# A decoder step with a mixture of experts on one core: bias sums and resident biases, samples and router in four column parts

## The reference, cut to what matters

```
proj = x @ w_in                              # queries, keys, values of two groups of 8 heads
o    = attention of both groups, each head RMS-normed and scaled
hx   = LayerNorm(alpha * x + o @ w_out) * ln1_g + ln1_b
logits = hx @ w_router + b_router            # 32 experts, the 4 best, softmax over their logits: comb
for each expert e:
    gu   = hx @ w_gate_up[e] + b_gate_up[e]          # 1024 x 2048
    act  = clamp(gate) * sigmoid(1.702 * gate) * (clamp(up) + 1)
    acc += comb[:, e] * (act @ w_down[e] + b_down[e]) # 1024 x 1024
y = LayerNorm(alpha * hx + acc) * ln2_g + ln2_b
```

## Time and profile before

| | |
|---|---|
| median of three executions | 1180.72 us |
| the profiled execution | 1180.89 us, of which the span is 1178.8 us |
| TensorE busy | 1121.9 us, 95% of the span |
| VectorE, ScalarE, GpSimd busy | 289.7, 203.8, 30.1 us |
| bytes moved | 454.21 MB, 385 GB/s over the span |
| mean granted TensorE clock | 0.99 of 2.4 GHz |

### The profile page before, as it was taken

One profiled execution on the slowest core, in us unless ns is written; L12 is line 12 of the kernel. 1 busy time (PEld: TensorE's weight loads), 2 busy tenths in 40 slices (PEclk: granted clock), 3 DMA queues, 4 the chain that ended last, 5 costly groups with the idle time before them and its releaser, 6 DMA issues.

```text
span 1178.8 us, 14219 instructions
## 1 busy us (share of the span) xinstructions
PE 1121.9 (95%) x5374; PEld 457.7 (39%) x5375; DVE 289.7 (25%) x707; ACT 203.8 (17%) x479; POOL 30.1 (3%) x65
## 2 busy tenths in 40 slices
PE   7999999899999999999999999999999999999986
PEld 6876764533333333333332323233333333333322
DVE  1543747602121211303030303030303030303113
ACT  1322412402020202021111111111111111111111
POOL 0110111000000000000000000000000000000001
PEclk9999999899999999999999999999999999999998
DMA  9857779668999999999999999999999999999992
GB/s 361 324 197 254 269 270 384 257 263 341 423 428 427 427 428 428 429 428 428 428 428 428 428 428 428 428 427 428 429 428 428 428 428 428 428 428 428 413 424 108
DMA packets 83399, 454.21 MB, mean 385 GB/s; under 512 B 7147, under 2 KB 20099, under 8 KB 36132
## 3 DMA queue, kind: packets, MB, share of 16 engines
q1 hardware_dynamic: 80866, 440.97, 90.5%
q0 software_dynamic: 1728, 10.75, 2.5%
q10 hardware_dynamic: 770, 2.03, 0.4%
HBM read 450.19 MB, written 11.93 MB: 392 GB/s over the span
## 4 chain that ended last, share of the span: by engine, by line
PE 65%; DMA 26%; SPq 5%; ACT 2%; DVE 1%; issue 1%
DMA ring<-in_w_gate_up 23%; PE bank L1083 19%; PE bank L1125 15%; PE bank L968 5%; PE bank L664 5%; PE bank L687 5%; SPq L445 3%; PE bank L851 3%; PE bank L690 2%; DMA ring<-in_w_down 2%; PE bank L1150 2%; PE bank L964 1%; SPq L455 1%; PE bank L804 1%; ACT xtok L1313 1%; ACT actT L1313 1%
## 5 line engine op out<-in xcount | busy, mean ns | idle before, releaser
L1083 PE MATMUL bank<-ring,xg 128*64 128x512 f32 x1904 | 422.8, 597 | 23.8 <-DMA ring<-in_w_gate_up 23.8
L1083 PEld LDWEIGHTS bank<-ring,xg 128*64 128x64 f32 x1904 | 132.0, 137 | 304.8 <-issue 252.3
L1125 PE MATMUL bank<-ring,actT 128*64 128x512 f32 x960 | 215.9, 597 | 3.8 <-ACT actT L1313 3.8
L1930 DVE TENSOR_TENSOR acc<-acc,bank 128x512 f32<-128x512 f32 x60 | 41.2, 687 | 509.3 <-PE bank L1150 509.3
L1458 ACT ACTIVATE sig<-gate 128x256 f32<-128x256 f32 x64 | 26.7, 416 | 545.6 <-DVE gate L1912 545.6
L1125 PEld LDWEIGHTS bank<-ring,actT 128*64 128x64 f32 x960 | 66.6, 137 | 121.5 <-issue 118.7
L1912 DVE TENSOR_SCALAR gate<-bank 128x256 f32<-128x256 f32 x64 | 26.8, 419 | 179.0 <-PE bank L1083 157.3
L687 PE MATMUL bank<-xT,wblk 128*128 128x288 f32 x256 | 67.1, 417 | 1.4 <-DMA wblk<-in_w_in 1.4
L1450 ACT ACTIVATE xg<-bank,small 128x128 f32<-128x128 f32 x128 | 48.1, 458 | 99.1 <-PE bank L664 99.1
L968 PE MATMUL bank<-hx,pick 128*128 128x512 f32 x128 | 61.6, 626 | 0.0
L1150 PE MATMUL bank<-ybuf,spread 128*128 128x512 f32 x120 | 58.3, 618 | 0.0
(11 more groups left out here) (245 smaller groups left out, 716.8 us busy)
## 6 DMA issues: line engine op xcount, KB each, us to landing
ring<-in_w_gate_up SPq DMA_DIRECT2D x119, 2048.0 KB, 29.2
ring<-in_w_down SPq DMA_DIRECT2D x63, 2048.0 KB, 31.5
ring<-in_w_gate_up SPq DMA_DIRECT2D x16, 1024.0 KB, 18.3
wblk<-in_w_in SPq DMA_DIRECT2D x12, 1024.0 KB, 7.4
kring<-in_cache_k_moba SPq DMA_DIRECT2D x16, 256.0 KB, 5.2
vring<-in_cache_v_moba SPq DMA_DIRECT2D x16, 256.0 KB, 5.0
out<-in_state_k_win POOLq DMA_DIRECT2D x8, 512.0 KB, 4.3
out<-in_state_v_win POOLq DMA_DIRECT2D x8, 512.0 KB, 4.9
```

The lines of the kernel that those rows point to most:

```text
L1083: ins = nc.tensor.matmul(bank[n][64 * e:64 * e + 64, :], xg[:, k, 64 * e:64 * e + 64], w[:, 2048 * e + 512 * n:2048 * e + 512 * n + 512], ...
L1125: ins = nc.tensor.matmul(bank[4 + half][64 * e:64 * e + 64, :], actT[:, j, 64 * e:64 * e + 64], w[:, at:at + 512], start=(j == 0), stop=(j ...
L1930: V.tensor_tensor(o, o, new, ALU.add).then_inc(S.added, 1)
```

## The change

The samples' value and out products go in four column parts. In `project` and as `out_samples`, which takes the place of `out_product` for the samples:

```
+                    for q in range(4):
+                        w = wblk[:, (b - 1 + q // 2) % 3, k, 128 * (q % 2):128 * (q % 2) + 128]
+                        ins = nc.tensor.matmul(out[NS * q:NS * q + NS, 256:384], xT[:, k, SEQ:T], w, start=(k == 0),
+                                               stop=(k == KC - 1), tile_position=(0, NS * q))
...
+        def out_samples(k):
+            for q in range(4):
+                ins = nc.tensor.matmul(bank[5][NS * q:NS * q + NS, 0:256], outT[:, k, SEQ:T],
+                                       wout[:, k, 256 * q:256 * q + 256], start=(k == 0), stop=(k == KC - 1),
+                                       tile_position=(0, NS * q))
+            return ins
```

ScalarE copies three of the four parts (`upper`), and VectorE's `v_rows` and `raw_sum` take four pieces instead of two. The router multiplies with its own columns as the stationary operand, in four column strips whose sum a second product with a stacked identity makes (`E` is 32):

```
+        def logits_parts(nth):
...
             for k in range(KC):
                 if k % 4 == 0:
                     pe.wait_ge(S.hxT_ready, 2 * nth + k // 4 + 1)
...
+                r = slice(E * (k % 4), E * (k % 4) + E)
+                ins = nc.tensor.matmul(bank[5][r, 128:128 + rows], wrt[:, k, :], outT[:, k, t0:t0 + rows], start=(k < 4),
+                                       stop=(k >= 4), tile_position=(0, E * (k % 4)))
+            ins.then_inc(S.parted, 1)
...
+        def logits_product(nth):
+            rows = TILES[ORDER[nth]][1]
+            pe.wait_ge(S.parts_ready, nth + 1)
+            nc.tensor.matmul(bank[5][0:rows, E * nth:E * nth + E], parts[:, 0:rows], keep[:, C_EYE:C_EYE + E], start=True,
+                             stop=True).then_inc(S.routed, 1)
...
+        def take_parts(nth):
+            rows = TILES[ORDER[nth]][1]
+            dve.wait_ge(S.parted, nth + 1)
+            V.tensor_copy(parts[:, 0:rows], bank[5][:, 128:128 + rows]).then_inc(S.parts_ready, 1)
```

The first pair's turned rows are awaited block by block, in the banks 6 and 7 in this order:

```
         def turn_slots(i, a):
-            pe.wait_ge(S.xtok_ready, i * 2 + 2)
+            early = isinstance(i, int) and i == 0
+            pe.wait_ge(S.xtok_ready, 1 + a if early else i * 2 + 2)
...
-                if isinstance(i, int) and i == 0 and k == 0:
+                if early:
+                    pe.wait_ge(*((S.xg_ready, k // 4 + 1) if k % 4 == 3 else (S.first_slots, 3 * (k // 4) + k % 4 + 1)))
+                if early and k == 0:
```

All biases of gate/up are loaded once, 32 rows for each of four column blocks, ahead of `load_v(3)`; `load_bias` and `next_bias` are gone. A pair's two rows are picked by the stationary operand, which VectorE writes for each pair, behind `pick_slots`:

```
+        for n in range(4):
+            sp.dma_start(bias_rows[E * n:E * n + E, :], b_gate_up[0, :, 512 * n:512 * n + 512]).then_inc(S.bias_in, 16)
...
+            pe.wait_ge(S.selected, i + 1)
             for n in range(4):
...
+                r = slice(E * n, E * n + E)
+                ins = nc.tensor.matmul(bank[n][:, :], sel[r, :], bias_rows[r, :], start=True, stop=False,
+                                       tile_position=(E * n, 0))
...
+        def select(i, p):
+
+            if not isinstance(i, int) or i > 0:
+                dve.wait_ge(S.bias_used, i)
+            V.tensor_copy(sel[:, :].rearrange("p (e s) -> p e s", e=2),
+                          eye[:, pair_of(p)].unsqueeze(2).broadcast_to([128, 2, SLOTS])).then_inc(S.selected, 1)
```

`select(0, 0)` stands ahead of `router_consts`. The second load of `ln_g` moves ahead of unit 9:

```
+        sp.wait_ge(S.added, 5)
+        sp.dma_start(ln_g[:, :], ln2_g[0:1, :].broadcast_to([128, D])).then_inc(S.ln2_in, 16)
         load_units(0, 0, range(9, UNITS))
-        sp.wait_ge(S.sums_scaled, 6)
-        sp.dma_start(ln_g[:, :], ln2_g[0:1, :].broadcast_to([128, D])).then_inc(S.ln2_in, 16)
-        next_bias(0)
```

```
-        gate_up(0, 0, 0, {1: turn_comb, 4: lambda: add_biases(0), 5: lambda: add_biases(1), 6: add_sample_biases})
+        gate_up(0, 0, 0)
...
+        def finish_with_biases(i, m, odd):
+
+            def first_slots():
+                turn_slots(i + 1, 0)
+                turn_comb()
+
+            def other_slots():
+                pe.wait_ge(S.actT_ready, i * 2 + 2)
+                turn_slots(i + 1, 1)
+                for j in range(2):
+                    add_biases(j)
+
+            def other_biases():
+                for j in range(2, 4):
+                    add_biases(j)
+                add_sample_biases()
+
+            gather(i + 1, i * 2)
+            turn_weights(i, i * 2 + 3)
+            turn_act(i, i * 2 + 4)
+            down(i, m, odd, {0: first_slots, 1: other_slots, 2: other_biases})
```

`add_biases(j)` is now one product of 33 rows and 512 columns into bank j; `add_sample_biases` waits for VectorE's first two sums and issues its eight products in two runs of four column strips. On ScalarE `take_comb` stands behind `take_turned(14)`. On VectorE, ahead of `add_mixed(14)`:

```
+        dve.wait_ge(S.added, 5 * PAIRS - 5)
+        add_biases()
+        dve.wait_ge(S.bias_added, 5)
```

More of the change, by code:

```diff
@@ L69, in constant_tables @@
     keep[:, C_ONE:C_ONE + 128] = 1
[L70 to L73, removed]
+    keep[:, C_IOTA:C_EYE] = np.arange(CHUNKS * SLOTS)
+    keep[p, C_EYE + p % E] = 1
     keep[p, C_HEAD + p // DS % H] = 1
@@ L167, in build_layer @@
     ln_gs, ln_bs = place("ln_gs", [128, 256]), place("ln_bs", [128, 256])
+    late_at = cursor[0]
+    parts = spread[:, 0:128]
     samp_x = place("samp_x", [NS, D])
+    bdn = hx[64:64 + E + 1, 2, :]
+    combT = place("combT", [128, T], at=late_at)[64:64 + E + 1, :]
     wrt = place("wrt", [128, KC, E], at=share_at)
@@ L294, in v_at @@
     def v_at(slot):
-        return sum((3 if n // 2 % 6 == 5 and n % 2 else 1) for n in range(slot + 1) if is_v(n))
+        return sum((5 if n // 2 % 6 == 5 and n % 2 else 1) for n in range(slot + 1) if is_v(n))
     def slot_of_tile(g, kind, j):
@@ L880, in out_part @@
                 pe.wait_ge(S.kstage_ready, 6)
-                out_first(2, range(4))
+                for k in range(4):
+                    out_samples(k)
         for slot in range(STEPS):
@@ L992, in _ @@
         for k in range(4, KC):
-            for half in range(2):
-                ins = out_product(2, half, k)
+            ins = out_samples(k)
         ins.then_inc(S.attended, 1)
@@ L1014, in _ @@
         ins.then_inc(S.attended, 1)
+        logits_parts(1)
+        out_product(1, 1, 4)
         logits_product(1)
-        for k in range(4, KC):
+        for k in range(5, KC):
             ins = out_product(1, 1, k)
@@ L1053, in add_sample_biases @@
-            ins.then_inc(S.spread_down, 1)
+            for q in range(4):
+                r, c = slice(NS * q, NS * q + NS), slice(256 * q, 256 * q + 256)
+                ins = nc.tensor.matmul(bank[1][r, 0:256], combT[:, SEQ:T], bdn[:, c], start=True, stop=True,
+                                       tile_position=(64, NS * q))
+            ins.then_inc(S.bias_sums, 1)
         def gather(i, turned_before):
@@ L1429, in _ @@
         act.wait_ge(S.attended, 1)
-        copy(upper[:, :], bank[5][NS:2 * NS, :]).then_inc(S.upper_ready, 1)
+        for q in range(1, 4):
+            copy(upper[:, q - 1, :], bank[5][NS * q:NS * q + NS, 0:256]).then_inc(S.upper_ready, 1)
         for nth in range(2):
@@ L1746, in raw_sum @@
             dve.wait_ge(S.attended, (2 + half, 4 + half, 1)[t])
[L1747 to L1748 removed]
+            if t == 2:
+                for q in (2 * half, 2 * half + 1):
+                    if q:
+                        dve.wait_ge(S.upper_ready, q)
+                    c = slice(256 * q, 256 * q + 256)
+                    o = upper[:, q - 1, :] if q else bank[5][0:NS, 0:256]
+                    ins = V.scalar_tensor_tensor(hx[0:n, t, c], hx[0:n, t, c], ALPHA, o, ALU.mult, ALU.add)
+                ins.then_inc(S.hx_raw, 1)
+                return
             c = slice(512 * half, 512 * half + 512)
[L1750 to L1751 removed]
+            V.scalar_tensor_tensor(hx[0:n, t, c], hx[0:n, t, c], ALPHA, bank[2 * t + half][:, :], ALU.mult,
+                                   ALU.add).then_inc(S.hx_raw, 1)
         def moments(nth, half):
```

184 lines of the change are left out of this document (79 added, 105 removed).

## The result

| | before | after |
|---|---|---|
| median, us | 1180.72 (1180.22 to 1181.76) | 1173.88 (1171.90 to 1174.39, 4 runs) |
| ratio to before | | 0.9938, 95% interval 0.9922 to 0.9953 |
| profiled execution, us | 1180.89 | 1174.04 |
| span, us | 1178.8 | 1172.1 |

The change brings 6.8 us, where 20.0 were forecast: 1173.9 against 1160.9, and outside the range of 1157 to 1167.

The account below looks back on a forecast made before the run. The weight stream was taken as the bound, with TensorE critical up to 244.4 us and through freed buffers to about 290; -9.2 - 6.0 - 1.2 - 5.2 + 1.6 = -20.0 us from 1180.9 gave 1160.9 us, range 1157 to 1167.

Parts of the forecast that it names:

- (a) to (f): Rivals: VectorE front 0.15, loop's turn 0.08, late work uncaught 0.07, full-clock gather 0.08, lower clock 0.02, stream gap stays 0.03.
- no stretch under 420 GB/s: Sign for the weight stream: from the issue of unit 9 to the last pair it never runs below 420 GB/s.
- part 3: Front: router product in column parts, counts placed later; the first full gather comes 2.0 us earlier.
- part 5: Pair 0: bias sums taken out, buffers free earlier, the stream's gap at 275 to 295 us closes: -6.0 us.
- Part 1: Front: samples' value product in four column parts, done twice, -3.4 us; a skill-based estimate gave 2.8 us.
- Part 2: Front: samples' out product in four parts, worth 0 since TensorE then waits for VectorE; two new holes.
- Part 4: Pair 0: first gate/up block needs one activation instead of all eight, starting about 1.1 us behind the gather: -3.2 us.
- The clock: TensorE's front: shorter hole gives the first block -1.1, new holes slow a full product +0.5: sum -0.6 us.
- rival (d): Front: TensorE's clock stays at 2.4 GHz through the gather, 6.12 becomes 3.7 us, total 1158.5 us; chance 0.08.
- Part 6: Stream: ln_g's load moved ahead of unit 9, -1.2 us; small bias loads gone, 15 x 0.35 = -5.2 us.
- Part 7: Pair 14 and tail: 5.2 us of moved TensorE work, 3.6 caught up in its waits: +1.6 us.
- The two tests named at the end of the prediction: The forecast is wrong if unit 9 is issued after 240 us, or the block 7 to 2 pitch stays at 34.65.

Follow-up runs that it names:

- a1: The changed kernel with 128 unused bytes ahead of the ring, so that its buffers start on multiples of 256 bytes: 1158.95 us.
- b3: a1 with ten products of 512 columns that nobody reads put behind blocks 4, 5 and 6 of pair 0: 1166.72 us.
- a4: a1 with the four two-row loads of a pair put back, into rows that nobody reads: 1163.61 us.
- c1: a1 with the samples' value product in two column parts, as before the change: 1162.82 us.
- b1: a1 with the samples' out product in two column halves, as before the change: 1158.92 us.
- c3: a1 with the router's product whole again and the counts of the known tiles ahead of the gather: 1160.25 us.
- b2: a1 with the first gate/up product of pair 0 waiting for all eight activations again: 1163.64 us.
- b4: a1 with the turned weights and bias sums moved from pair 14 to pair 7: 1157.87 us.
- c2: a1 with ring buffers 0 to 3 on multiples of 256 bytes and 4 to 7 put 128 bytes past one: 1163.02 us.
- c4: a1 with one unread product of 512 columns in each of TensorE's two holes behind the samples' out product: 1158.88 us.

## Why the prediction was wrong

The step that failed is a sentence in the first part that was carried through all others: "19.60 / 4 = 4.90 us for 2 MB", used again as "seven units before it, 34.3 us at 4.90" for the kernel after. The pitch was taken to be a property of the chip and of the load's shape. It also depends on where the buffers start, and the change moved them. Nothing in the trace of before could show that price, but its cause stood in the diff, in declarations that were passed over and so costed at zero without a word. None of the rivals (a) to (f) had it. Nor could the sign named for the stream catch it: "no stretch under 420 GB/s" lets 421 pass. The price was 0.07 us for each of 168 units, 11.8 us, and about 15 us in all.

With the ring back in place, the forecast of all that I did cost comes out 2 us from the time: 1158.95 against 1160.9. Span against span, `a1` (1157.1) and before (1178.8):

| stretch | before | a1 | difference | forecast |
|---|---|---|---|---|
| to the issue of unit 9 | 244.40 | 233.25 | -11.15 | -9.2 |
| from there to block 7 of pair 10 | 597.48 | 587.15 | -10.33 | -6.0 - 1.2 - 11 x 0.35 = -11.05 |
| on to block 7 of pair 14 | 236.58 | 235.20 | -1.38 | -4 x 0.35 = -1.4 |
| on to the end | 100.34 | 101.50 | +1.16 | +1.6 |
| sum | | | -21.7 | -20.05 |

That the sum comes so near is in part luck, as errors cancel: the front gave more than forecast by its clock and less by part 3, the gap of part 5 was worth 7.0 and not 6.0 (`b3`), and the 15 sets of bias loads 3.3 in the profile of `a4` and not 5.2.

The kernel after against `a1`: +2.20 to unit 9 (the first keys are turned at 22.73 and not 20.54: those loads go into the ring as well; they are at 20.6 to 21.5 in the nine other profiles with the ring on, the kernel before among them, and at 21.7 to 22.7 in the three with it off), +11.83 on to block 7 of pair 14, +0.97 behind it, 15.0 in all.

Point by point:
- Part 1, -3.4: right, 3.5 by `c1`. The value product takes 1.96 us, 1.93 in the row it was read from; the other estimate, 2.8 us from the losses between column tiles (by its own factor of 1.3 it is 2.6), was too low.
- Part 2, 0: right, by `b1`. The named holes came as said (1.16 and 1.70 for 1.1 and 2.1); the full product behind them at the lower clock was given one chance in three and came in six of ten.
- Part 3, -2.0: the sign right, the size 1.1 by `c3`.
- Part 4, -3.2: right, 3.1, by `b2`, and the 1.7 us of the first block's clock with it, which the forecast had at two in three.
- The clock: net -0.6 was too small. The gather at full clock, rival (d) with 0.08, came in every profile of the changed front: -2.4 us. The first block's 1.7 came back too and the full product at 200 lost as much. So the clock gave 2.4 for 0.6, and 0.85 more in the small products ahead of the gather (`c3`); with part 3's 0.9 too many that leaves 0.2 of the 1.95 us in the table's first row, and the first keys came 0.2 earlier. Why the gather kept its clock is open: it isn't the router's parts (`c3`), nor the wait by blocks (`b2`).
- Part 5, -6.0: the gap closed; the same TensorE time put back costs 7.0 to 7.8 by `b3`.
- Part 6: that the bias loads cost the stream is shown, 4.7 us between the medians of `a4` and `a1` for 5.2. But 15 x 0.35 took the price of a late pair for all: behind unit 9 the profile has 3.3. That ln_g's 1.2 went can only be read from the sum.
- Part 7: the extra work takes 5.4 us (0.44 for the turn, 1.92 and 1.91 for the sums, 1.13 for the samples'; forecast 5.2) and is caught up but for 1.2 us; of these `b4` gives back 0.5.
- The first reading of the earlier trace rows was generous: 427 to 429 GB/s stands in slices 12 to 37, 26 slices of 29.5 us, some 770 us and not 860. No term of the sum used it.

The two tests named at the end of the prediction told what they should: unit 9 was before 240, and the stretch from block 7 to 2 did read 34.79 and not 34.65 or 34.3. Only that number, read against the pitch inside a pair, separates a load that stayed from a stream that slowed.

## What to carry to other kernels

When a change touches declarations, add up the addresses behind them: here a shorter table and a new tile moved the weight buffers by 128 bytes and took 15 of 22 us back. In a kernel bound by its loads, read the pitch of one transfer before and after, ahead of all else: a flat GB/s line at another height with the same DMA share is a changed transfer and not a changed order. And put the buffers of the main stream on multiples of 256 bytes; of the kernels tried `a1` costs one line and beats both, 1158.95 us.

## What the runs showed of the hardware

- Loads of 8 KB rows into SBUF run at 428 GB/s where the row starts on a multiple of 256 bytes and at 421 to 422 where it starts 64 or 128 bytes past one; with half of the buffers off it was 426 (`c2`, 300 to 600 us).
- Four loads of two rows and 4 KB each, 16 KB, hold a saturated stream up for 0.35 us where TensorE waits for each unit (59.15 against 58.80 us a pair); the first eight such sets cost 0.84 us together.
- TensorE's granted clock can fall behind holes of 1.16 and 1.70 us, with 3.7 us of full products between them, in six of ten profiles of the same code; and behind eight narrow products (sixteen records, 1.1 us) without any hole, in two of eleven (`c2`, `c4`). Full products of 3.7 us then take 5.3 to 5.4, in one profile 6.7.
